# The entry of the feed-forward input stages in another order, with the third weight sum of iteration 0 made by accumulating DMAs

## What is computed

```
x = x + 1/2 * SwiGLU_1(RMSNorm(x))            # 2048 -> 2 x 5632 -> 2048
h = RMSNorm(x); P = h @ W_in                  # 8 dilated-attention heads, 8 differential heads
x = x + concat(heads) @ W_out
x = x + 1/2 * SwiGLU_2(RMSNorm(x))

swiglu: gate, up = split(h @ w_in);  (silu(gate) * up) @ w_out
```

## Time and profile before

| what | value |
|---|---|
| median of 3 runs | 1783.69 us |
| profiled execution | 1783.53 us |
| its span, first to last instruction | 1781.6 us |
| PE busy | 1771.4 us, 99% |
| DVE busy | 1537.5 us, 86% |
| ACT busy | 1142.8 us, 64% |
| POOL busy | 113.6 us, 6% |
| accumulating DMAs (queue q0) | 52.43 MB, 16.3% of 16 engines' span |
| all other DMAs (queue q1) | 351.02 MB, 55.3% |

### The profile page before, as it was taken

The page is one execution under the profiler, slowest core; times in us unless marked ns, Lnnn a source line. Parts: engine busy times, 40 slices in busy tenths (PEclk is TensorE's granted clock), DMA queues, the critical chain, the costliest instruction groups (busy, mean ns, idle before and its releaser), DMA issues.

```text
span 1781.6 us, 21421 instructions
## 1 busy us (share of the span) xinstructions
PE 1771.4 (99%) x8107; PEld 1468.8 (82%) x8107; DVE 1537.5 (86%) x1656; ACT 1142.8 (64%) x1397; POOL 113.6 (6%) x153
## 2 busy tenths in 40 slices
PE   9999999999999999999999999999999999999999
PEld 8788888888888888888888888788888888888887
DVE  7999999999899887657666666999999999889886
ACT  7677777777665564556556655677767777756553
POOL 0000001000000000211010000000000000000000
PEclk9999999999999999999999999999999999999999
DMA  9889999997656566655555445799998998744654
GB/s 352 236 264 271 286 276 273 268 263 213 213 188 236 202 222 211 196 167 166 166 166 179 152 166 176 248 272 272 278 286 259 274 287 234 236 177 171 249 194 142
DMA packets 189318, 404.82 MB, mean 227 GB/s; under 512 B 7824, under 2 KB 8864, under 8 KB 186400
## 3 DMA queue, kind: packets, MB, share of 16 engines
q1 hardware_dynamic: 177664, 351.02, 55.3%
q0 software_dynamic: 11520, 52.43, 16.3%
q10 hardware_dynamic: 32, 0.01, 0.0%
HBM read 348.91 MB, written 2.10 MB: 197 GB/s over the span
## 4 chain that ended last, share of the span: by engine, by line
PE 98%; DVE 1%; issue 0%; ACT 0%; DVEq 0%; POOL 0%; ACTq 0%; POOLq 0%
PE acc L600 27%; PE acc L606 13%; PE turn L685 12%; PE acc L685 9%; PE acc L666 8%; PE turn L689 6%; PE acc L689 5%; PE acc L671 4%; PE turn L806 3%; PE acc L806 2%; PE turn L636 1%; PE turn L809 1%; PE acc L809 1%; PE turn L925 1%; PE turn L600 1%; PE turn L946 1%
## 5 line engine op out<-in xcount | busy, mean ns | idle before, releaser
L1067 ACT ACTIVATE w_hi<-b 128x1024 fp32r<-128x1024 f32 x300 | 310.8, 1058 | 108.4 <-PE acc L671 63.0
L1463 DVE TENSOR_TENSOR w_lo<-b,w_hi 128x1024 fp32r<-128x1024 f32 x300 | 351.8, 1214 | 19.8 <-ACT w_hi L1067 19.8
L1453 DVE TENSOR_TENSOR w_lo<-w_raw,w_hi 128x1024 fp32r<-128x1024 f32 x147 | 181.1, 1241 | 118.9 <-ACT w_hi L1041 118.4
L1081 ACT ACTIVATE w_hi<-w_raw 128x1024 fp32r<-128x1024 f32 x184 | 193.8, 1059 | 130.3 <-PE acc L606 95.0
L1041 ACT ACTIVATE w_hi<-w_raw 128x1024 fp32r<-128x1024 f32 x146 | 154.5, 1060 | 176.5 <-PE acc L606 161.4
L1473 DVE TENSOR_TENSOR w_lo<-w_raw,w_hi 128x1024 fp32r<-128x1024 f32 x184 | 222.6, 1221 | 39.7 <-ACT w_hi L1081 36.4
L600 PE MATMUL acc<-w_hi,h_hi 128*128 128x512 f32 x480 | 190.1, 396 | 0.0
L600 PE MATMUL acc<-w_hi,act_hi 128*128 128x512 f32 x480 | 187.1, 390 | 0.0
L600 PE MATMUL acc<-w_hi,h_lo 128*128 128x512 f32 x480 | 187.1, 390 | 0.0
L600 PE MATMUL acc<-w_hi,act_lo 128*128 128x512 f32 x480 | 186.7, 389 | 0.0
L1067 ACT ACTIVATE w_hi<-t 128x1024 fp32r<-128x1024 f32 x120 | 124.5, 1060 | 51.5 <-PE acc L671 33.2
(11 more groups left out here) (241 smaller groups left out, 3628.8 us busy)
## 6 DMA issues: line engine op xcount, KB each, us to landing
b<-in_ffn_w_in SPq DMA_DIRECT2D x80, 1536.0 KB, 8.5
w_raw<-in_ffn_w_out SPq DMA_DIRECT2D x88, 1024.0 KB, 5.8
w_raw<-in_ffn_w_in SPq DMA_DIRECT2D x50, 1024.0 KB, 7.3
w_raw<-in_w_in SPq DMA_DIRECT2D x48, 1024.0 KB, 5.0
b<-t POOLq DMA_DIRECT2D x20, 1024.0 KB, 6.9
w_raw<-in_w_out SPq DMA_DIRECT2D x16, 1024.0 KB, 5.0
b<-b POOLq DMA_DIRECT2D x20, 512.0 KB, 6.4
t<-b POOLq DMA_DIRECT2D x20, 512.0 KB, 5.8
```

The costliest lines, as they stand in the source:

```text
L1067: nc.scalar.activation(w_hi[:, u % RING, 0:count, :], in_raw(piece)[:, k0:k0 + count, :], ACT.Copy).then_inc(hi_ready, 1)
L1081: nc.scalar.activation(w_hi[:, u % RING, :, :], src, ACT.Copy).then_inc(hi_ready, 1)
L1453: nc.vector.tensor_tensor(w_lo[:, slot, 0:count, :], first_raw(raw)[:, k0:k0 + count, :], w_hi[:, slot, 0:count, :].bitcast(F32), ALU.subt ...
L1463: nc.vector.tensor_tensor(w_lo[:, u % RING, 0:count, :], in_raw(piece)[:, k0:k0 + count, :], w_hi[:, u % RING, 0:count, :].bitcast(F32), A ...
```

## The change

Five things change, in both stages unless said.

1. The third sum of iteration 0 is made by DMA alone: DVE's two `third_sum` instructions are left out for i = 0, and POOL issues one more DMA, k-tiles 0 to 3 of b_12 += b_22, 1024 KB, ahead of the one for k-tiles 4 and 5. P7's first two units wait for it (`lone_sum_landed`). `sum_ready` now counts two less per stage. Iterations 1 to 9 are as before.
2. `wide` is made in three pieces of 4 k-tiles, each as early as its activations are split, where it was two pieces of 6 (IN1) or one of 12 (IN2).
3. The signed sums come earlier in IN2 (ahead of unit 9's w_lo; the norm factor moves behind unit 10's), and DVE does not wait for each piece of `wide` on the spot.
4. In IN1 `split_sums` moves ahead of unit 13's w_lo on DVE; on ACT `round_in_sums` moves from behind unit 13's w_hi to ahead of unit 12's.
5. `second_sum` waits for b_22's landing itself, which `third_sum` did before it.

```diff
-SUMS = IN_SUMS * IN_LOOPS + 4 * len(PERIODS)
+LOOP_SUMS = IN_SUMS * IN_LOOPS - 2
+SUMS = LOOP_SUMS + 4 * len(PERIODS)
...
+        def sums_before(n, i):
+
+            return n * SUMS + IN_SUMS * i - (2 if i else 0)
...
                     elif name == "P7" and k0 == KT:
                         act.wait_ge(part_sum_landed[0], 16 * done)
+                    elif name == "P7" and i == 0:
+                        act.wait_ge(lone_sum_landed, 16 * (n + 1))
                     elif name == "P7":
...
-                    split_hi(s_in, 9, 13, PARTS_D)
+                    split_hi(s_in, 9, 12, PARTS_D)
+                    round_in_sums(n)
+                    split_hi(s_in, 12, 13, PARTS_D)
...
                 split_hi(s_in, 13, 14, PARTS_D)
-                if n == 0:
-                    round_in_sums(n)
                 split_in_hi(s_in, n, 0, RING)
...
-                third_sum(n, i, 0, UK)
+                if i:
+                    third_sum(n, i, 0, UK)
                 split_in_lo(s_in, FIRST[i - 1, "UB"], LAST[i - 1, "UB"] + 1)
-                third_sum(n, i, UK, KT)
+                if i:
+                    third_sum(n, i, UK, KT)
...
-            def activation_wide(first, last):
-
-                to, k = slice(KS * first, KS * last), slice(K_PLAIN + KS * first, K_PLAIN + KS * last)
-                link(nc.vector.tensor_tensor(wide[:, to, :], h_hi[:, k, :].bitcast(F32), h_lo[:, k, :].bitcast(F32),
-                                             ALU.add))
+            def activation_wide(k0, k1, turned):
+
+                dve.wait_ge(turn_split, turned)
+                nc.vector.tensor_tensor(wide[:, k0 - K_PLAIN:k1 - K_PLAIN, :], h_hi[:, k0:k1, :].bitcast(F32),
+                                        h_lo[:, k0:k1, :].bitcast(F32), ALU.add).then_inc(wide_made, 1)
...
                 if n == 0:
                     split_lo(s_in, 5, 6, PARTS_D)
+                    activation_wide(2 * KT, 3 * KT, 3)
                     scale_norm(3)
-                    split_lo(s_in, 6, 7, PARTS_D)
-                    dve.wait_ge(turn_split, 3)
-                    activation_wide(0, 1)
-                    split_lo(s_in, 7, 8, PARTS_D)
-                    dve.wait_ge(turn_split, 4)
-                    blocks = activation_wide(1, 2)
+                    split_lo(s_in, 6, 8, PARTS_D)
+                    activation_wide(3 * KT, KD, 4)
                     split_lo(s_in, 8, 10, PARTS_D)
-                    signed_sums(s_raw, *blocks)
+                    signed_sums(s_raw, *blocks_of(3))
                     split_lo(s_in, 10, 11, PARTS_D)
                     norm_factor(2 * n)
-                    split_lo(s_in, 11, 14, PARTS_D)
+                    split_lo(s_in, 11, 13, PARTS_D)
                     split_sums(n)
+                    split_lo(s_in, 13, 14, PARTS_D)
                 else:
-                    split_lo(s_in, 4, 8, PARTS_D)
+                    split_lo(s_in, 4, 5, PARTS_D)
+                    activation_wide(KT, 2 * KT, splits(r0 - 2))
+                    split_lo(s_in, 5, 6, PARTS_D)
+                    activation_wide(2 * KT, 3 * KT, splits(r0 - 1))
+                    split_lo(s_in, 6, 8, PARTS_D)
                     turn_split_lo(r0 - 1, h_hi, h_lo, 12, 0)
+                    split_lo(s_in, 8, 9, PARTS_D)
+                    activation_wide(3 * KT, KD, splits(r0))
+                    signed_sums(s_raw, *blocks_of(6))
+                    split_lo(s_in, 9, 11, PARTS_D)
                     norm_factor(2 * n)
-                    split_lo(s_in, 8, 10, PARTS_D)
-                    blocks = activation_wide(0, 2)
-                    split_lo(s_in, 10, 11, PARTS_D)
-                    signed_sums(s_raw, *blocks)
                     split_lo(s_in, 11, 12, PARTS_D)
                     split_sums(n)
                     split_lo(s_in, 12, 14, PARTS_D)
...
             split_lo(IN1, 2, 4, PARTS_D)
             dve.wait_ge(turn_hi, 2)
             scale_lo(1, range(2, 4), turn_split)
+            activation_wide(KT, 2 * KT, 2)
             split_lo(IN1, 4, 5, PARTS_D)
...
                     pool.wait_ge(block_landed[B22 - B11], 16 * (done + 1))
-                    pool.wait_ge(sum_ready, SUMS * n + IN_SUMS * i + 2)
+                    pool.wait_ge(sum_ready, sums_before(n, i) + 2)
+                    if i == 0:
+                        nc.gpsimd.dma_start(b_12[:, 0:KT, :], b_22[:, 0:KT, :],
+                                            accum_op=ALU.add).then_inc(lone_sum_landed, 16)
                     nc.gpsimd.dma_start(b_12[:, KT:KS, :], b_22[:, KT:KS, :],
                                         accum_op=ALU.add).then_inc(part_sum_landed[0], 16)
```

More of the change, by code:

```diff
@@ L340, in hybrid_layer_kernel @@
         s_raw_ready = sem("s_raw_ready")
+        wide_made = sem("wide_made")
         s_hi_ready = sem("s_hi_ready")
@@ L345, in hybrid_layer_kernel @@
         part_sum_landed = [sem(f"part_sum_landed{n}") for n in (3, 2)]
+        lone_sum_landed = sem("lone_sum_landed")
         first_landed = [sem(f"first_landed{i}") for i in range(2)]
@@ L521, in ffn @@
                     load(down, a, k, KT, 2, at + X2 + 1)
-                    sp.wait_ge(sum_ready, SUMS * n + IN_SUMS * IN_LOOPS + 4 * (m + 1))
+                    sp.wait_ge(sum_ready, SUMS * n + LOOP_SUMS + 4 * (m + 1))
                     load(down, a, j, KT, 0)
@@ L1048, in split_in_hi @@
                     u = UNIT[s_in] + IN_FIRST + v
-                    sums, done = SUMS * n + IN_SUMS * i, IN_LOOPS * n + i + 1
+                    sums, done = sums_before(n, i), IN_LOOPS * n + i + 1
                     if name == "P5":
@@ L1058, in split_in_hi @@
                     elif name == "P6":
-                        act.wait_ge(sum_ready, sums + (6 if k0 else 5))
+                        act.wait_ge(sum_ready, sums + (6 if k0 else 5) - (0 if i else 2))
                     elif name == "P4":
@@ L1075, in split_out_hi @@
                     if made:
-                        act.wait_ge(sum_ready, SUMS * n + IN_SUMS * IN_LOOPS + made)
+                        act.wait_ge(sum_ready, SUMS * n + LOOP_SUMS + made)
                     else:
@@ L1157, in copy_m1 @@
                 else:
-                    act.wait_ge(sum_ready, SUMS * n + IN_SUMS * IN_LOOPS + 4 * (m + 1))
+                    act.wait_ge(sum_ready, SUMS * n + LOOP_SUMS + 4 * (m + 1))
                 act.wait_ge(units_used, UNIT[s_out] + period_at(m) + Q1 + 1)
@@ L1562, in third_sum, with second_sum @@
                 dve.wait_ge(block_landed[B22 - B11], 16 * (IN_LOOPS * n + i + 1))
-                dve.wait_ge(sum_ready, SUMS * n + IN_SUMS * i + 2)
+                dve.wait_ge(sum_ready, sums_before(n, i) + 2)
                 weight_sum(b_12[:, k0:k1, :], b_22[:, k0:k1, :], b_12[:, k0:k1, :], ALU.add)
-            def second_sum(s_in, i, k0, k1):
+            def second_sum(s_in, n, i, k0, k1):
+                dve.wait_ge(block_landed[B22 - B11], 16 * (IN_LOOPS * n + i + 1))
                 dve.wait_ge(lo_ready, UNIT[s_in] + IN_FIRST + LAST[i, "P5"] + 1)
@@ L1634, in hidden_last, with blocks_of @@
                 split_out_lo(s_out, 3, 4)
-            def activation_wide(first, last):
-                to, k = slice(KS * first, KS * last), slice(K_PLAIN + KS * first, K_PLAIN + KS * last)
-                link(nc.vector.tensor_tensor(wide[:, to, :], h_hi[:, k, :].bitcast(F32), h_lo[:, k, :].bitcast(F32),
-                                             ALU.add))
+            def activation_wide(k0, k1, turned):
+                dve.wait_ge(turn_split, turned)
+                nc.vector.tensor_tensor(wide[:, k0 - K_PLAIN:k1 - K_PLAIN, :], h_hi[:, k0:k1, :].bitcast(F32),
+                                        h_lo[:, k0:k1, :].bitcast(F32), ALU.add).then_inc(wide_made, 1)
+            def blocks_of(made):
+                dve.wait_ge(wide_made, made)
                 return [wide[:, KS * half:KS * (half + 1), t * P:(t + 1) * P] for half in range(2) for t in range(TT)]
@@ L1745, in begin_products @@
                 u0, at = period_at(m), UNIT[s_out] + period_at(m)
-                made = SUMS * n + IN_SUMS * IN_LOOPS + 4 * m
+                made = SUMS * n + LOOP_SUMS + 4 * m
                 b_11, b_12, b_22 = w_raw[:, 0, 0:UK, :], w_raw[:, 1, 0:UK, :], w_raw[:, 1, UK:KT, :]
```

6 lines of the change are left out of this document (3 added, 3 removed).

## The result

| | before | changed |
|---|---|---|
| median, us | 1783.99 (20 runs, 1783.23 to 1784.99) | 1786.28 (20 runs, 1785.27 to 1788.51) |
| profiled execution, us | 1783.53 | 1788.51 |
| its span, us | 1781.6 | 1786.6 |
| DVE busy, us | 1537.5 | 1533.4 |
| queue q0, MB | 52.43 | 54.53 |

The ratio is 1.0014, with a 95% interval of 1.0008 to 1.0021: some 2.3 us slower, and within the 0.2% that was set as no change. The profiled execution of the changed kernel is the slowest of its 20, 2.2 us over their median.

The account below looks back on a forecast made before the run. PE was taken as the bound, busy 1771.4 of 1781.6 us. Old stalls -6.2, new stalls +3.0 and +2.4, ACT's queue +1.2, late DVE +0.6 gave +1.0: 1784.7 us from 1783.69, range 1779.6 to 1788.0.

Parts of the forecast that it names:

- All 6.2 us of old stalls go: PE's stalls in iteration 0 of IN1 and IN2, from low halves late on DVE, vanish: -6.2 us.
- The wide pieces and the s sums cost nothing on the path: At both stages' start, wide's three pieces fall into DVE's waits and ACT's rounding is ready before PE wants it: no cost.
- the front of IN2: Rival: signed sums ahead of unit 9's low half make IN2's front stall 1 to 2 us, 1786; chance 0.04.
- The new stall stands at P6's last unit: In iteration 0, t_1's part queues behind the new sum on POOL, so PE stalls 3.0 us in IN1, 2.4 in IN2.
- The three sums take 18.6 us: POOL's three accumulating DMAs at iteration 0, from first issue to landing in t_1: 18.6 us, bounds 18.2 and 20.2.
- the pair (13.0): POOL's two 512 KB sums at IN1's entry in the kernel before, first issue to last landing: 13.0 us.
- what 1024 KB add to it (5.6): Extra time of the new 1024 KB sum in POOL's queue: 5.6 us taken, between 5.2 and 7.2.
- The point from which this was to decide for slower, 19.9: Length of the three sums from which the shared-engines rival (1787.9 us, chance 0.16) would make the result slower: 19.9 us.
- the prediction's own formula: Stall at P6's last unit: t_1's landing plus ACT's and DVE's work, against when PE wants the low half; 3.0 and 2.4 us.
- 1.2 us for ACT's queue and 0.6 for a late DVE: After P6's stall, P7's halves come late behind ACT's queue, 1.2 us, and DVE is late afterwards, 0.3 us per stage.
- head delay gone: Rival: POOL's first sum lands without the entry's 3.2 us delay, 1777.5 us; chance 0.10 both stages, 0.12 one.
- the other 1777.5 of the prediction: Total by the Trainium skill's transfer cost, where the three sums take 15.4 us and nothing waits; the prediction did not follow it.

Follow-up runs that it names:

- e5: The changed kernel with the new 1024 KB accumulating DMA taken out and nothing in its place, so the layer is not computed: 1777.48 us.
- e2: The kernel before, in its old order, with the new 1024 KB DMA in place of DVE's third sum of iteration 0: 1791.62 us.
- e3: The changed kernel, but POOL issues at iteration 0 the sum into t_1 first, then the two into b_12: 1786.93 us.
- e8: The changed kernel run once more, unchanged, to look at its clock: median 1786.53 us, profiled execution 1787.23 us.
- e6: The changed kernel without the new DMA; DVE makes the third sum of iteration 0 later, among P6's low halves: 1778.26 us.
- e9: The changed kernel, but at iteration 0 the next b_11 load is issued behind POOL's second sum, not ahead of its first: 1787.40 us.
- e4: The changed kernel, but SyncE holds the next b_11 load and the G0 load at iteration 0 until t_1's sum has landed: 1788.50 us.
- e7: The changed kernel, but only the next b_11 load is held at iteration 0 until t_1's sum has landed; G0's is not: 1784.58 us.
- e1: The changed kernel's new order alone, without the new DMA; DVE makes the third sum of iteration 0 ahead of UB and P5: 1778.96 us.

## Why the prediction was right, and what it had wrong

The forecast was 1784.7 with a range of 1779.6 to 1788.0; the median of 1786.28 lies in it, and no change held. The forecast had 1.0 us more than before, and the medians differ by 2.3. Step by step:

- **All 6.2 us of old stalls go: right.** POOL's first issue came at 52.73 for a forecast of 52.7; e5, with the rest taken away, came to 1777.48 for the 1777.5 that this step gives. The kernel before gave 1784.46 beside e5, so by the medians the step is 7.0; between the two profiled executions it is 1783.53 - 1777.48 = 6.05.
- **The wide pieces and the s sums cost nothing on the path: right.** No wait of PE ahead of UB or P5, and none at the front of IN2, so that rival falls too.
- **The new stall stands at P6's last unit and follows from the place in POOL's queue: right.** e2 shows it with the old order, and e3 moves it away by turning the queue around.
- **The three sums take 18.6 us: too short.** 19.9 and 19.4 in the profiled execution, 19.0 and 19.1 in e8. Too little was put either on the pair (13.0) or on what 1024 KB add to it (5.6). In IN1 the pair alone took 14.0 in e5 and 12.9 in e6, so the new sum adds 5.9 or 7.0, and the record does not part the two. In the changed kernel the last two sums take 3.3 each in the queue for 512 KB, where 2.6 was taken for an undisturbed one. The point from which this was to decide for slower, 19.9, was too high, for want of the clock below: the execution with 19.9 and 19.4 took 1788.5. The stalls by the prediction's own formula are 3.0 + 1.3 and 2.4 + 0.8 = 7.5 us at those lengths; the low half of the unit started 4.4 and 3.3 late (75.07 and 1163.19, wanted at 70.7 and 1159.85), so the formula holds, and with the 3.4 us of half clock these 7.7 make 11.1 of the 11.24.
- **1.2 us for ACT's queue and 0.6 for a late DVE: not there.** No wait of PE names them in either profile, and the sum just made has no room for them. Probably ACT and DVE catch up while PE runs at half clock; no run shows it without that.
- **The clock: missing.** The full clock was granted throughout in the kernel before, and I took a stall to cost its length. In both profiled executions of the changed kernel each stall costs 1.7 us more, 3.4 in all; in most executions, by their mean granted clock, at most one of the two did. For the profiled execution the mended sum is 1.0 + 2.1 for the longer sums - 1.8 + 3.4 = 4.7 of the 5.0 measured. Errors of opposite sign stand in it, and that the median came within 1.6 us of 1784.7 is in part luck.
- **The rival "head delay gone" did not come about, but its mechanism exists:** e9 takes it away by issuing the load 2.5 us later. It was worth nothing, since its price assumed that nothing else waits for the DMA engines. The time of 1777.5 for it was wrong by 10 us. The same fault is in the other 1777.5 of the prediction, for three sums of 15.4 us, and in e4's expectation.

What the prediction did not have at all is the sum over queues: it priced one transfer in one queue, and asked who waits behind it there. e3, e4, e7, e9 and the changed kernel itself all make some engine wait, 6.3 to 10.2 us over e6. That no order does better is not shown; five were tried.

## What to carry to other kernels

An addition that moves from an engine into an accumulating DMA is not free because the engine was late: here 1024 KB cost 5.3 us of all 16 DMA engines, twice a load's price, to spare VectorE 2.4 us. Before making the move, look at the DMA share of the stretch; here it stood near 1.0 (0.98 from 54 to 90 us of the changed kernel), and whatever came next on any queue was late. Look first for a place where the engine idles later on: the same sum made 14 us later on VectorE (65.70 in e6, 51.91 in e1) gave 1778.26. And when a change has two halves, run each alone: the order by itself is 4.8 us faster than before, which the DMA hid.
